# Split weights at places that change from strip to strip, on one NeuronCore

## The reference

```python
# layer 1: T = 528 token rows (16 meta + 512)
h = rms_norm(x, norm1_w)
(rq, rk, rv, rg, dq, dk, dv, cb, cc, cx, gates) = [h @ w_in[:, s:e] for s, e in column_bounds()]
ret, diff, conv = retention(...), diff_attention(...), cb * short_conv(cc * cx, conv_w)
merged = g0 * (ret @ w_branch[0]) + g1 * (diff @ w_branch[1]) + g2 * (conv @ w_branch[2])
x = x + merged @ w_out
x = x + square(relu(rms_norm(x, norm2_w) @ w_up)) @ w_down
# layer 2: again 16 meta tokens in front
#   stick-breaking attention and gated linear attention from h @ w_in_2, each projected and gated,
#   their sum @ w_o, then a gated feed-forward part with w_ffn_up, w_ffn_gate, w_ffn_down
```

## Time and profile before

| what | value |
|---|---|
| median of 3 runs | 2102.28 us (2102.26 to 2102.3) |
| the profiled execution | 2102.32 us |
| its span, first to last instruction | 2100.5 us |
| TensorE clock granted, mean | 0.999 of full speed |
| PE busy | 2087.2 us, 99% |
| weight loads busy (beside PE) | 1850.4 us, 88% |
| VectorE, ScalarE, GpSimd busy | 1244.4, 831.4 and 164.4 us |
| DMA | 203.36 MB, 97 GB/s |

### The profile page before, as it was taken

The page is one execution under the profiler, slowest core; times in us unless marked ns, Lnnn a source line. Parts: engine busy times, 40 slices in busy tenths (PEclk is TensorE's granted clock), DMA queues, the critical chain, the costliest instruction groups (busy, mean ns, idle before and its releaser), DMA issues.

```text
span 2100.5 us, 33898 instructions
## 1 busy us (share of the span) xinstructions
PE 2087.2 (99%) x13662; PEld 1850.4 (88%) x13662; DVE 1244.4 (59%) x1847; ACT 831.4 (40%) x1305; POOL 164.4 (8%) x146
## 2 busy tenths in 40 slices
PE   9999999999999999999999999999999999999998
PEld 8998988898888788899898888999999998889897
DVE  6775444565555555777665666367855567546364
ACT  4333222433444443434434566343424344222233
POOL 0012000030000000232120000022300000000000
PEclk9999999999999999999999999999999999999999
DMA  4343221522222233332323221231133222322322
GB/s 151 111 167 114 86 76 61 199 82 83 73 68 71 96 106 99 109 111 81 110 91 100 81 92 60 82 122 59 54 140 105 91 80 91 97 94 90 100 91 100
DMA packets 53563, 203.36 MB, mean 97 GB/s; under 512 B 6960, under 2 KB 7344, under 8 KB 52288
## 3 DMA queue, kind: packets, MB, share of 16 engines
q1 hardware_dynamic: 49248, 177.56, 26.3%
q10 hardware_dynamic: 3232, 20.80, 2.5%
q0 software_dynamic: 960, 3.24, 0.5%
HBM read 190.96 MB, written 10.62 MB: 96 GB/s over the span
## 4 chain that ended last, share of the span: by engine, by line
PE 93%; DVE 4%; ACT 2%; issue 0%; DMA 0%; SPq 0%; DVEq 0%; ACTq 0%
PE ps L2174 69%; PE ps L2297 7%; PE ps L2773 5%; PE ps L2639 1%; PE ps L2421 1%; PE ps L2446 1%; PE ps L2374 1%; PE ps L2705 1%; PE ps L2545 1%; DVE kk_r L1827 1%; PE ps L2460 1%; ACT kk L966 1%; ACT kk L967 1%; PE ps L2683 0%; PE ps L2526 0%; PE ps L2353 0%
## 5 line engine op out<-in xcount | busy, mean ns | idle before, releaser
L556 ACT ACTIVATE wh<-wraw 128x1024 fp32r<-128x1024 f32 x284 | 300.3, 1057 | 730.7 <-PE ps L2174 612.5
L1234 DVE TENSOR_TENSOR wl<-wraw,wh 128x1024 fp32r<-128x1024 f32 x298 | 365.6, 1228 | 132.6 <-ACT wh L556 129.0
L2174 PE MATMUL ps<-xh,wh 128*128 128x264 f32 (+1 forms) x1800 | 325.3, 325 | 0.6 <-DVE tmp L1267 0.5
L2174 PE MATMUL ps<-xl,wh 128*128 128x264 f32 (+1 forms) x1800 | 317.2, 321 | 0.0
L2174 PE MATMUL ps<-xh,wl 128*128 128x264 f32 (+1 forms) x1800 | 316.8, 320 | 0.0
L2174 PEld LDWEIGHTS ps<-xh,wh 128*128 128x128 f32 x1800 | 264.4, 188 | 30.1 <-issue 2.4
L2174 PEld LDWEIGHTS ps<-xl,wh 128*128 128x128 f32 x1800 | 265.2, 188 | 25.7
L2174 PEld LDWEIGHTS ps<-xh,wl 128*128 128x128 f32 x1800 | 265.2, 188 | 25.3
L2174 PE MATMUL ps<-bh,wh 128*128 128x264 f32 (+1 forms) x1296 | 231.7, 322 | 0.3 <-ACT wh L556 0.2
L2174 PE MATMUL ps<-bl,wh 128*128 128x264 f32 (+1 forms) x1296 | 227.9, 319 | 0.0
L2174 PE MATMUL ps<-bh,wl 128*128 128x264 f32 (+1 forms) x1296 | 227.8, 319 | 0.0
(11 more groups left out here) (532 smaller groups left out, 2776.8 us busy)
## 6 DMA issues: line engine op xcount, KB each, us to landing
wraw<-weights_dram SPq DMA_DIRECT2D x299, 512.0 KB, 3.6
qq<-weights_dram SPq DMA_DIRECT2D x12, 512.0 KB, 4.5
kk<-weights_dram SPq DMA_DIRECT2D x12, 512.0 KB, 4.4
hf<-tables_dram POOLq DMA_DIRECT2D x12, 264.0 KB, 3.0
res<-x_t_dram SPq DMA_DIRECT2D x4, 528.0 KB, 7.2
res<-x_t_dram ACTq DMA_DIRECT2D x1, 2112.0 KB, 9.2
res_dram<-res ACTq DMA_DIRECT2D x1, 2112.0 KB, 6.4
mrg_dram<-mrg ACTq DMA_DIRECT2D x1, 2112.0 KB, 8.7
```

What stands on the lines that cost most here:

```text
L556: nc.scalar.activation(wh[:, slot], wraw[:, slot], ACT.Copy).then_inc(hi_done, 1)
L1234: nc.vector.tensor_tensor(wl[:, slot], wraw[:, slot], wh[:, slot].bitcast(F32), ALU.subtract)\
L2174: last = nc.tensor.matmul(o, w[:, slot, c, :], a[:, c, tok], start=(k == 0), stop=(k == len(steps) - 1))
```

## The change

`wh` and `wl` get 64 more values per slot, and a strip's split parts may start at `PLACE[n]` values (0, 8, ..., 56; 32 bytes each) into the slot. A slot is now 4352 bytes instead of 4096, a whole multiple of 256 as before, so what lies behind keeps its place. `strip_at` gives the view of a strip, and ScalarE, VectorE and TensorE all use it.

Of 139 strips over all tokens 122 get another place; the other 17 keep place 0, as their turn in the table is 0. By place: 20 strips at 8 (distances 96 and 64), 12 at 16 (128, 96), 17 at 24 (160, 128), 29 at 32 (192, 160), 8 at 40 (224, 192), 14 at 48 (0, 224), 22 at 56 (32, 0). That is 5856 matmuls of 264 columns. As the table goes by pairs of strips in most groups, ten strips over 512 tokens in `ret_qkv` and `diff_qkv` move too, and the first strip of each `glu..down`, 312 matmuls of 512 columns in all. The Strassen parts stay.

```diff
+PLACE = [0] * NSTRIP
+for _name in ("ret_qkv", "diff_qkv", "sb_main", "sb_proj", "gla_lr", "gla_main", "gla_gates"):
+    for _n in range(dict(PHASES)[_name]):
+        PLACE[START[_name] + _n] = 8 * (_n // 2 % 8)
+for _k in range(24):
+    PLACE[START["conv_in"] + _k] = (8, 24, 0, 32, 56, 0)[_k % 6]
+for _k in range(8):
+    PLACE[START["gla_proj"] + _k] = PLACE[START["w_o"] + _k] = (32, 48)[_k % 2]
+for _g, _n in enumerate(FFN2_GROUPS):
+    for _k in range(_n):
+        PLACE[START[f"glu{_g}up"] + 2 * _k] = (32, 56)[_k % 2]
+    PLACE[START[f"glu{_g}down"]] = 32
...
-    return base + k + step * i, (base + k) // 2 + (step // 2) * i, (base + k) % 2
+    return base + k + step * i, (base + k) // 2 + (step // 2) * i, Slot(base + k)
...
+def strip_at(w, n, slot):
+    o = PLACE[n if isinstance(n, int) else slot.first]
+    return w[:, int(slot), o:o + KC * P].rearrange("p (k n) -> p k n", k=KC)
...
-        wh, wl = sb("wh", [P, 2, KC, P], F32R), sb("wl", [P, 2, KC, P], F32R)
+        wh, wl = (sb(n, [P, 2, KC * P + 64], F32R) for n in ("wh", "wl"))
...
-                nc.scalar.activation(wh[:, slot], wraw[:, slot], ACT.Copy).then_inc(hi_done, 1)
+                nc.scalar.activation(strip_at(wh, n, slot), wraw[:, slot], ACT.Copy).then_inc(hi_done, 1)
...
-                with act.Fori(0, count // 2) as i:
+                with act.Fori(0, count // 2 - 1) as i:
                     for j in range(2):
                         split_hi(*pos(B, j + 1, i))
+                for k in (count - 1, count):
+                    split_hi(*pos(B, k))
...
-                        last = nc.tensor.matmul(o, w[:, slot, c, :], a[:, c, tok], start=(k == 0),
+                        last = nc.tensor.matmul(o, strip_at(w, number, slot)[:, c, :], a[:, c, tok], start=(k == 0),
```

More of the change, by code:

```diff
@@ L74, with __new__ @@
 NSTRIP = sum(p[1] for p in PHASES)
-def pos(base, k=0, i=0, step=2):
-    return base + k + step * i, (base + k) // 2 + (step // 2) * i, (base + k) % 2
+PLACE = [0] * NSTRIP
[10 more added lines that the diff above has]
+    PLACE[START[f"glu{_g}down"]] = 32
+def pos(base, k=0, i=0, step=2):
+    return base + k + step * i, (base + k) // 2 + (step // 2) * i, Slot(base + k)
+class Slot(int):
+    def __new__(cls, first):
+        slot = int.__new__(cls, first % 2)
+        slot.first = first
+        return slot
+def strip_at(w, n, slot):
+    o = PLACE[n if isinstance(n, int) else slot.first]
+    return w[:, int(slot), o:o + KC * P].rearrange("p (k n) -> p k n", k=KC)
 def flat(ap):
@@ L174, in build @@
         S3 = A21
-        st_w = ([wh[:, k].rearrange("p k n -> p (k n)") for k in range(2)] + [flat(vtr)[:, 4 * D:5 * D]],
-                [wl[:, k].rearrange("p k n -> p (k n)") for k in range(2)] + [flat(xrowsr)[:, 0:D]])
+        st_w = ([wh[:, k, 0:KC * P] for k in range(2)] + [flat(vtr)[:, 4 * D:5 * D]],
+                [wl[:, k, 0:KC * P] for k in range(2)] + [flat(xrowsr)[:, 0:D]])
         t_raw_row = flat(xrows)[:, D:2 * D]
@@ L585, in _ @@
                     act.wait_ge(w_loaded[0], 16)
-                    nc.scalar.activation(wh[:, 0, 0:2], wraw[:, 0, 0:2], ACT.Copy).then_inc(first_hi, 1)
+                    nc.scalar.activation(strip_at(wh, 0, 0)[:, 0:2], wraw[:, 0, 0:2], ACT.Copy).then_inc(first_hi, 1)
                 if c == 1:
-                    nc.scalar.activation(wh[:, 0, 2:KC], wraw[:, 0, 2:KC], ACT.Copy).then_inc(hi_done, 1)
+                    nc.scalar.activation(strip_at(wh, 0, 0)[:, 2:KC], wraw[:, 0, 2:KC], ACT.Copy).then_inc(hi_done, 1)
             n_hi += KC
@@ L1233, in split_lo @@
                 dve.wait_ge(hi_done, n + 1)
-                nc.vector.tensor_tensor(wl[:, slot], wraw[:, slot], wh[:, slot].bitcast(F32), ALU.subtract)\
+                nc.vector.tensor_tensor(strip_at(wl, n, slot), wraw[:, slot], strip_at(wh, n, slot).bitcast(F32), ALU.subtract)\
                     .then_inc(lo_done, 1)
@@ L1278, in _ @@
                     dve.wait_ge(first_hi, 1)
[L1279 removed]
+                    nc.vector.tensor_tensor(strip_at(wl, 0, 0)[:, 0:2], wraw[:, 0, 0:2],
+                                            strip_at(wh, 0, 0)[:, 0:2].bitcast(F32), ALU.subtract)\
                         .then_inc(first_lo, 1)
@@ L2096, in _ @@
                 B = START[f"glu{g}down"]
-                with dve.Fori(0, n_g // 2) as i:
+                with dve.Fori(0, n_g // 2 - 1) as i:
                     for j in range(2):
                         split_lo(*pos(B, j + 1, i))
+                for k in (n_g - 1, n_g):
+                    split_lo(*pos(B, k))
                 for t in range(4):
@@ L2196, in product @@
                             (ps[:, 2 * p[2], :], slice(NM, T))
-                        ins = nc.tensor.matmul(o, w[:, p[2], c, :], a[:, c, tok], start=(c == 0 and w is wh and a is xh),
+                        ins = nc.tensor.matmul(o, strip_at(w, p[0], p[2])[:, c, :], a[:, c, tok], start=(c == 0 and w is wh and a is xh),
                                                stop=(c == KC - 1 and a is xl))
@@ L2249, in first_strip @@
                         for k in range(2):
-                            last = nc.tensor.matmul(ps[:, k, 0:HALF], w[:, 0, c, :], a[:, c, HALF * k:HALF * k + HALF],
+                            last = nc.tensor.matmul(ps[:, k, 0:HALF], strip_at(w, 0, 0)[:, c, :], a[:, c, HALF * k:HALF * k + HALF],
                                                     start=(c == 0 and w is wh and a is xh),
@@ L2587, in strip_by_halves @@
                         for c in range(KC):
-                            last = nc.tensor.matmul(ps[:, k, 0:HALF], w[:, slot, c, :],
+                            last = nc.tensor.matmul(ps[:, k, 0:HALF], strip_at(w, n, slot)[:, c, :],
                                                     a[:, c, HALF * k:HALF * k + HALF], start=(w is wh and a is bh and c == 0),
@@ L2638, in _ @@
                             for k in range(2):
-                                last = nc.tensor.matmul(ps[:, z + k, 0:HALF], w[:, slot, 4 * o + c, :],
+                                last = nc.tensor.matmul(ps[:, z + k, 0:HALF], strip_at(w, n, slot)[:, 4 * o + c, :],
                                                         a[:, c, HALF * k:HALF * k + HALF],
@@ L2767, in chunk_products @@
             def chunk_products(g, c, n_g, tiles, w, a, halves_of=(0, 1)):
-                slot = (START[f"glu{g}down"] + c) % 2
+                n = START[f"glu{g}down"] + c
+                slot = n % 2
                 for t in tiles:
@@ L2773, in chunk_products @@
                         last = nc.tensor.matmul(ps[:, 2 * t + h, :], a[:, c, NM + P * t:NM + P * t + P],
-                                                w[:, slot, 4 * h:4 * h + 4, :].rearrange("p k n -> p (k n)"),
+                                                strip_at(w, n, slot)[:, 4 * h:4 * h + 4, :].rearrange("p k n -> p (k n)"),
                                                 start=first, stop=(c == n_g - 1 and w is wl), skip_group_check=True)
```

3 lines of the change are left out of this document (2 added, 1 removed).

## The result

The changed kernel takes 2108.85 us (median of 7 runs, 2108.64 to 2108.99), the one before in the same rounds 2102.29 us (7 runs, 2102.11 to 2102.4): a ratio of 1.0031, interval 1.0019 to 1.0043, +6.6 us. The forecast was 2109.

What follows compares the result with a forecast made beforehand. PE, busy 99% of the span, was taken to bound the kernel. 2102.3 + 7.2 us for 264 columns, all else 0, gave 2109.5, stated as 2109 us; own range 2105 to 2115, eight in ten 2090 to 2122.

Steps and rivals of the forecast that it cites:

- The bound: Whole kernel: PE busy 99% of the span, 93% of the chain; only one matmul's cost can move the time much.
- Splits, unrolled loops, wider slots at 0: ACT copies and DVE subtractions hidden beside a strip's matmuls, loop ends beside PE's work, other tensors' places kept: 0 us.
- Place counts: Weights' place against moving columns counts by several ns per matmul, read from 256-column steps of 113.3 to 120 ns.
- Sum for 264 columns: 5856 strip matmuls: ns over columns/2.4, averaged over halves, minus today's 10.0; summed 151 ns x 48 = +7.2 us.
- The step that failed: Excess is step time over columns/2.4; a strip takes its halves' mean: 13.3 ns at 0, 10.0 at 32 and 64.
- the middle, 8.9: Distance 192 in the strips: excess between 6.7 and 11 ns with 256 columns, taken as 8.9.
- The fast step: 256 columns at nonzero distances: 113.8 and 113.3 ns against 117.9 and 117.5, begun after four matmuls at distance 0 and a few more.
- 512 columns taken as nothing: 240 matmuls in ten strips, -1.6 to +1.2 us, and 72 in `glu..down`, -0.5 to +0.4 us; both taken as nothing.
- Signs to look for: Next profile: 264-column mean 282 to about 283.5 ns, 512-column mean 389; `w_o` and `gla_proj` (places 32, 48) 120 and 122 ns.
- Rival A: Strips leave the slow step: all nonzero places fast, -13.6 us, 2089; half of that, 2095; chance 0.35.
- Rival B: 264-column strips: distances near 128 cost 18 ns as in L2558, neighbours too: +18.5 us, 2121; chance 0.14.
- Rival C: Strips keep 120.0 ns, set by the pace of loads and issue, not by operand starts: 2102; chance 0.13.

Runs made afterwards that it cites:

- the rows put in: Kernel before plus 832 matmuls at 1718 us, product read by nobody, weights at eight starts: pairs of 264 columns took 120.0 to 122.7 ns a step.

## Why the prediction was right, and where it was not

- **The bound.** "The only thing that can move the time by much is what one matmul costs PE": right. PE's busy time and the span grew by the same 6.5 us, and no wait cost more time than before.
- **Splits, unrolled loops, wider slots at 0.** Right, shown by the kernel with all strips at the old place (2102.15).
- **Place counts, and today's pair of distances is among the cheapest.** Right, shown by the rows put in: 120.0 to 122.7 ns with the same data, shapes and neighbours.
- **Sum for 264 columns, +7.2 us.** Measured +6.0 (5.55, 0.44, 0.08 and 0.04 at four lines, less the 0.14 of the first strip). That the sum is close is luck, as two errors cancelled: places 8, 48 and 56 were given 84 ns x 48 = 4.0 us and cost 0.2 at L2207; place 32 was given nothing and costs 2.4 there. The total, 2109 against 2108.85, had luck once more: the 264 columns were sized 1.2 us too high, and the 512 columns (+1.25 us) were left out.
- **The step that failed** is the excess by distance and its mean over the halves. The 192 was taken from steps with 256 columns, "the middle, 8.9", which made the pair 192, 160 free; with 264 columns that pair takes 122.1 ns. The 13.3 at distance 0 came from 256 and 512 columns; in a pair with 32 or 224 it costs 264 columns nothing. A price does not carry over from one number of columns to another (512 are cheapest at distance 0, 256 at 224), nor do two add up to a pair. What did carry over is that the neighbourhood of 128 is the dear one, which paid for places 16 and 24: 2.5 and 2.2 ns predicted, 2.2 and 2.7 in undisturbed strips.
- **The fast step.** The prediction let it begin after four matmuls at distance 0 (172.60). There were twelve; two rows ahead of it were not shown:

```profile
171.65 0.64 PE L2297 MATMUL ps<-xh,wh 128*128 128x256 f32 x4
172.12 0.64 PE L2297 MATMUL ps<-xl,wh 128*128 128x256 f32 x4
```

They take 118.8 ns a step, so distance 0 has more than one price too. And it is no chance: L2297 has ten blocks of such matmuls in before, and in every one the 256 columns at a nonzero distance take 117 to 118 ns (waits aside) up to the first twelve at distance 0, and 113 to 114 from the fifth matmul behind these on. So a step depends on what ran before it too, and the "middle, 8.9" for distance 192 is the mean of two such histories, neither of which is that of a strip over all tokens.
- **512 columns taken as nothing.** Mis-sized: +0.9 us for the ten strips, +0.35 for `glu..down`. The prediction's bounds, +1.2 for the strips and +0.4 for `glu..down`, held; the middle was too low, since the excess at distance 0 was read as a high price and is the lowest for this shape (227.2 against 229.0 to 234.5).
- **Signs to look for.** The 264-column mean rose from 282 to 283 and 284, as said; the 512-column mean was to stay at 389 and is 390. `w_o` and `gla_proj` were said to show 120 and 122: they show 122.1 and 120.4, at the other places.
- **Rival A** (some place, or changing between places, gives the fast step): not so. No place, cut, start off the grid or sequence that was tried went below 120.0 ns for a pair; changing among cheap places gave 2102.91. The fast 113.3 ns of 256 columns never came in the rows put in, whose 256-column steps were 116.7 to 120.2; but none of these stood right behind 256 columns at distance 0, where it begins in the kernel.
- **Rival B** (18 ns near 128): the direction was right, the size was not; the dearest pair costs 2.6 ns more than today's, the dearest single distance 3.4. The 18 of the earlier trace rows belonged to three matmuls of other shapes, and it is no mark of 128: in the rows put in, 512 columns are 19 ns over their 213.3 at distance 128, but 20 to 21 at 32, 64, 96 and 160.
- **Rival C** (nothing): refuted by old place against changed table, 2102.15 and 2108.85, with nothing else between them.

Open: what the two reads share (the runs show only that the price goes with the distance between their starts, and in part with what ran before), why some history brings the fast step at L2297, and what splits rows at one pair of distances into 121.7, 122.5 and 123.3 ns. The stretches put in were measured in one run each. The remedies tried end at 120.0 ns, so no version beats the kernel before.

## What to carry to other kernels

In a kernel that is bound by PE, the place of the weights against the moving columns within 256 bytes is worth reading before the layout of a buffer is changed: for 264 columns it moved a step by up to 2.2% (120.0 to 122.7 ns), for 512 by up to 3.2% (227.2 to 234.5). Measure it with the very shape and the very sequence of moving parts, as a row of dummy matmuls between two fixed points of the kernel; prices of another number of columns or of single halves mislead. And when a sum comes out right, look at its terms: here two were wrong by 2.4 and 3.8 us in opposite directions.

## What the runs showed that was not expected

- Of the three shapes put in, the 512-column matmul is the most sensitive, and not in proportion to the distance: 227.2 ns at distance 0, 229.0 at 192, 232.6 to 234.5 at the other six.
- In undisturbed strips at place 48 the two halves take 123 and 117 ns in turn, at place 8 122 or 123 and 118 or 117: a half can be well under 120.0, but the pair never was. Over all the places, off-grid starts and cuts tried, 120.0 ns was met again and again as the floor for a pair.
- Starts off the 32-byte grid cost up to 2.4 ns even where both neighbours on it are cheap: 121.6 ns with the weights 4 bytes further than today, 122.5 with 16 bytes, against 120.1 today and 120.3 with 32.
